# VectorE's weight step moved behind the work of its slot, and five smaller changes, in a four-layer model on one core

## What is computed

```python
def rms_norm(x, g):
    y = xf * lax.rsqrt(jnp.mean(xf * xf, axis=-1, keepdims=True) + EPS)
    return (y * g).astype(x.dtype)

def layer_c(...):                                   # layer 1
    u, gate = jnp.split(rms_norm(x, norm_g) @ w_in, 2, axis=-1)
    z = jax.nn.gelu(s5_ssm(u, ...))
    z = z * jax.nn.sigmoid(z @ glu_w + glu_b)
    return x + (z * jax.nn.silu(gate)) @ w_out

def first_block(...): ...                           # layers 0 and 1
    return rms_norm(x, final_norm_g)

def second_block(...):                              # layers 2 and 3
    for l in range(DEPTH):
        proj = jnp.einsum("bsd,de->bse", rmsnorm(x, norm_w[l]), w_in[l])
        ...                                         # ssd, conformer and attention branches
        x = x + jnp.einsum("bse,ed->bsd", concatenate([y_ssd, y_cfm, y_att]), w_out[l])

def ssd_chunked(x, dt, A, B, C):                    # 16 heads of 64, chunks of 128
    a_cs = jnp.cumsum(a, axis=-1)
    decay_in = segsum_exp(a_cs)
    y_diag = jnp.einsum("bcgls,bcgjls,bcsgjp->bclgjp", cb, decay_in, xdt)
```

## Time and profile before

| | us |
|---|---|
| median of three runs | 3628.29 |
| lowest and highest | 3622.89, 3630.3 |
| the profiled execution | 3625.47 |
| its span | 3623.7 |
| PE busy | 3464.2 |
| VectorE busy | 2127.2 |
| ACT busy | 1288.7 |
| GpSimd busy | 150.4 |

### The profile page before, as it was taken

One profiled execution on the slowest core, in us unless ns is written; L12 is line 12 of the kernel. 1 busy time (PEld: TensorE's weight loads), 2 busy tenths in 40 slices (PEclk: granted clock), 3 DMA queues, 4 the chain that ended last, 5 costly groups with the idle time before them and its releaser, 6 DMA issues.

```text
span 3623.7 us, 42976 instructions
## 1 busy us (share of the span) xinstructions
PE 3464.2 (96%) x15890; PEld 2770.9 (76%) x15890; DVE 2127.2 (59%) x3122; ACT 1288.7 (36%) x2013; POOL 150.4 (4%) x100
## 2 busy tenths in 40 slices
PE   8899999999999999999989999998999999999899
PEld 6687887777777888788878876776777887677677
DVE  6755546677655645434244775566755476565774
ACT  4233324444332233423152224324423223532442
POOL 2000000000020000000050000000002000000000
PEclk9899999999999999999999999998999999999899
DMA  4233335566665555645443442344446343334445
GB/s 163 100 123 123 112 130 180 175 235 217 227 212 183 177 176 185 202 168 198 152 161 117 164 137 99 114 139 164 151 160 216 106 166 132 104 122 161 141 156 198
DMA packets 286129, 574.58 MB, mean 159 GB/s; under 512 B 61392, under 2 KB 101088, under 8 KB 285408
## 3 DMA queue, kind: packets, MB, share of 16 engines
q1 hardware_dynamic: 285920, 571.83, 47.0%
HBM read 440.65 MB, written 131.07 MB: 158 GB/s over the span
## 4 chain that ended last, share of the span: by engine, by line
PE 52%; issue 23%; DVE 13%; ACT 6%; DMA 3%; DVEq 2%; POOLq 1%; SPq 0%; ACTq 0%
PE bank L542 34%; PE bank L541 11%; DVE weights_low L467 3%; ACT weights_high L394 2%; DVE arena L1963 2%; ACT arena L1905 1%; POOLq L453 1%; DVE residual_in L2037 1%; DVE arena L1958 1%; DMA convert_in<-x 1%; PE bank L1076 1%; DVEq L2541 1%; ACT arena L1902 1%; DVE act_low L525 1%; PE bank L988 1%
## 5 line engine op out<-in xcount | busy, mean ns | idle before, releaser
L542 PE MATMUL bank<-act_high,weights_high 128*128 128x512 f32 x3584 | 1449.3, 404 | 77.1 <-DVE stream_out L514 34.7
L542 PE MATMUL bank<-act_low,weights_high 128*128 128x512 f32 x3584 | 1416.8, 395 | 0.0
L467 DVE TENSOR_TENSOR weights_low<-weights_raw,weights_high 128x1024 fp32r<-128x1024 f32 x528 | 656.9, 1244 | 1122.0 <-ACT weights_high L394 1119.4
L394 ACT ACTIVATE weights_high<-weights_raw 128x1024 fp32r<-128x1024 f32 x528 | 558.1, 1057 | 1517.7 <-PE bank L542 1256.4
L542 PE MATMUL bank<-act_high,weights_low 128*128 128x512 f32 x3584 | 962.8, 389 | 0.0
L542 PEld LDWEIGHTS bank<-act_high,weights_high 128*128 128x128 f32 x3584 | 686.1, 191 | 248.0 <-issue 54.4
L542 PEld LDWEIGHTS bank<-act_low,weights_high 128*128 128x128 f32 x3584 | 685.7, 191 | 138.5 <-issue 2.9
L542 PEld LDWEIGHTS bank<-act_high,weights_low 128*128 128x128 f32 x3584 | 672.8, 188 | 140.1
L541 PE MATMUL bank<-weights_high,act_high 128*128 128x512 f32 x640 | 255.4, 399 | 23.3 <-DVE stream_out L480 18.1
L541 PE MATMUL bank<-weights_high,act_low 128*128 128x512 f32 x640 | 250.6, 392 | 0.0
L2037 DVE SCALAR_TENSOR_TENSOR residual_in<-residual_in,arena 128x512 f32<-128x512 f32 x240 | 180.4, 752 | 20.8 <-issue 1.8
(11 more groups left out here) (318 smaller groups left out, 2879.4 us busy)
## 6 DMA issues: line engine op xcount, KB each, us to landing
weights_raw<-in_w_all SPq DMA_DIRECT2D x528, 512.0 KB, 3.3
convert_in<-mix SPq DMA_DIRECT2D x80, 256.0 KB, 4.2
fm_b<-stream_out SPq DMA_DIRECT2D x72, 256.0 KB, 2.3
mix<-arena SPq DMA_DIRECT2D x64, 256.0 KB, 2.7
x_part<-stream_out SPq DMA_DIRECT2D x48, 256.0 KB, 2.2
residual_in<-x_part SPq DMA_DIRECT2D x12, 1024.0 KB, 7.0
x<-stream_out SPq DMA_DIRECT2D x48, 256.0 KB, 2.6
convert_in<-x SPq DMA_DIRECT2D x48, 256.0 KB, 3.9
```

Source lines behind the costliest of these rows:

```text
L394: e.activation(WH[:, t % 3, :], RAW[:, t % 3, :], ACT.Copy).then_inc(wh_ready, 1)
L467: e.tensor_tensor(WL[:, t % 3, :], RAW[:, t % 3, :], WH[:, t % 3, :].bitcast(F32), ALU.subtract).then_inc(wl_ready, 1)
L542: return e.matmul(bank[s][:, :], a[:, s * P:(s + 1) * P], h, start=start, stop=stop)
```

## The change

1. VectorE's slot becomes: evacuation, converts, take(t), WL(t+2).
2. Ahead of layer 2 each tile is squared once. GpSimd adds the squares, and VectorE adds them times the square of the gain to the second sum, one operation for each tile.
3. The constants of S5 get buffers of their own, stand in 27 slots between 10 and 75, and GLA doesn't wait for them.
4. k of S5 is written to four groups of 32 partitions (columns of the array), and one ACT copy of 128x256 takes it out.
5. SSD: the cumulative sums of all heads are formed once for each layer; each head picks its row with one rounded matmul of 512 columns; y of a pair of heads is formed together, the instructions alternating between the two column halves; a head has six slots and four buffers of decay.
6. The residual is loaded tile by tile; where a pass with a residual follows another, each tile's load is issued right behind the store of the tile before.

```diff
-                if t + AHEAD < NU:
-                    weights_dve(e, t + AHEAD)
                 for n in BY_SLOT.get(t, ()):
                     convert_dve(e, n)
                 take(t)
+                if t + AHEAD < NU:
+                    weights_dve(e, t + AHEAD)
```

```diff
-                square_act(e, SQ_AT[ph] + (2 * k if ph == 5 else k), x)
-                if ph == 5:
-                    square_act(e, SQ_AT[ph] + 2 * k + 1, x, GAIN[:, 2, k:k + 1])
+                square_act(e, SQ_AT[ph] + k, x)
...
+            if ph == 5:
+                sq = SQ_AT[ph] + k
+                e.wait_ge(sq_ready, sq + 1)
...
+                    e.scalar_tensor_tensor(ACC2, SQ[:, sq % 2, :], GAIN[:, 6, k:k + 1], ACC2, ALU.mult, ALU.add
+                                           ).then_inc(sq_gained, 1)
```

```diff
-        PREP_STEPS = 12
+        PREP_SLOTS = [*range(10, 22), *range(29, 33), *range(43, 46), *range(56, 59), 69, 70, 71, 74, 75]
+        PREP_STEPS = len(PREP_SLOTS)
...
-                e.wait_ge(*pr_d.at("done"))
```

```diff
             for g in range(S5_G):
-                mm = e.matmul(mid[2 + g // 4][0:S5_C, (g % 4) * P:(g % 4 + 1) * P], sw_vb[:, g, P - S5_C:],
+                r = slice(32 * (g % 4), 32 * (g % 4) + 32)
+                mm = e.matmul(mid[2][r, (g // 4) * P:(g // 4 + 1) * P], sw_vb[:, g, P - 2 * S5_C:],
                               sw_cp[:, g, 0:P], start=True, stop=True)
```

```diff
-            for b in range(TB):
-                mm = e.matmul(mid[h % 2][:, b * P:(b + 1) * P], sd_ab[h % 2][:, b, :], TRI[:, :], start=True, stop=True)
...
+            e.matmul(mid[h % 2][:, :], SMW[:, h, :], ROWS_R[:, :], start=True, stop=True).then_inc(*sd_pacs.mark("acs"))
+            yield
+            yield
+            yield
+            if h % 2:
...
+                for b in range(TB):
+                    for n in (h - 1, h):
+                        r = slice(64 * (n % 2), 64 * (n % 2) + 64)
+                        mm = e.matmul(mid[2 + k % 2][r, b * P:], sd_xdt[:, b, n * 64:(n + 1) * 64], packed(sd_e[n % 4], b),
+                                      start=b == 0, stop=b == TB - 1)
```

```diff
                 e.dma_start(dst, OUTB[:, s, :]).then_inc(out_stored, 16)
+                if follows(q + 1):
+                    residual_sp(e, q + 1, s)
```

More of the change, by code:

```diff
@@ L960, in sw_act @@
                 e.wait_ge(sw_kst, 16 * b)
-            for n in range(2):
-                ins = e.activation(sw_k[0:S5_C, 4 * n:4 * n + 4, :],
-                                   mid[2 + n][0:S5_C, :].rearrange("p (g n) -> p g n", g=4), ACT.Copy)
-            ins.then_inc(*sw_a.mark("kc"))
+            e.activation(two_d(sw_k), mid[2][:, 0:2 * P], ACT.Copy).then_inc(*sw_a.mark("kc"))
             e.wait_ge(*sw_d.at("arg", b))
@@ L1675, in build @@
         sd_e = [A(PACK[4]) for _ in range(2)]
-        sd_ab = [A(TB, P) for _ in range(2)]
         sd_x, sd_z, sd_y = A(2, L), A(2, L), A(2, L)
@@ L1680, in build @@
         sd_w, sd_dsk, sd_pick = A(12, 5), A(8), A(16)
+        after_conv = Arena(0, 6 * L)
+        sd_e += [after_conv(PACK[4]) for _ in range(2)]
+        sd_two = sd_x[:, 0, :].rearrange("p (b n) -> p b n", b=TB)
         conv = Arena(SD_E, SD_E + 2 * PACK[4])
@@ L1710, in ssd_pre_pe @@
             e.matmul(mid[0][:, 0:64], TRI[:, :], a2, start=True, stop=True)
-            e.matmul(mid[0][:, 64:128], ONES[:, :], a2, start=True, stop=True).then_inc(*sd_tp.mark("sums"))
+            e.matmul(mid[0][:, 64:128], ONES[:, :], a2, start=True, stop=True)
+            for b in range(TB):
+                mm = e.matmul(mid[1][:, b * P:(b + 1) * P], sd_two[:, b, :], TRI[:, :], start=True, stop=True)
+            mm.then_inc(*sd_tp.mark("sums"))
             yield
@@ L1761, in ssd_pre_dve @@
                 e.drain()
-            e.drain().then_inc(*sd_td.mark("bias"))
+            e.tensor_copy(ROWS_R[:, :], mid[1][:, :])
+            e.drain()
+            low = slice(64, P)
+            e.tensor_tensor(ROWS_R[low, :], mid[1][low, :], ROWS_R[low, :].bitcast(F32), ALU.subtract)
+            e.drain().then_inc(*sd_td.mark("rows"))
             yield
@@ L1953, in ssd_dve @@
             e.wait_ge(*sd_pacs.at("acs", t))
-            ee, ps = sd_e[h % 2], mid[h % 2]
-            if h >= 2:
-                e.wait_ge(*sd_py.at("y", t - 2))
+            ee, ps = sd_e[h % 4], mid[h % 2]
+            if h >= 4:
+                e.wait_ge(*sd_py.at("y", l * 8 + k - 2))
+            if h == 2:
+                for n in range(2):
+                    e.wait_ge(sd_xst[n], 16 * (l * 4 + 4))
             for b in range(TB):
@@ L2577, in _ @@
                     weights_sp(e, t + 5)
-                if UNITS[t][0] in XR_TURN and FIRST[UNITS[t][0]] == t:
-                    residual_sp(e, UNITS[t][0])
+                q = UNITS[t][0]
+                if q in XR_TURN and FIRST[q] == t and not follows(q):
+                    residual_free_sp(e, q)
+                    for s in range(4):
+                        residual_sp(e, q, s)
                 for n in BY_SLOT.get(t + 1, ()):
```

182 lines of the change are left out of this document (104 added, 78 removed).

## The result

| | before, us | changed, us |
|---|---|---|
| median of four runs each | 3629.3 | 3683.7 |
| lowest and highest | 3622.9, 3630.7 | 3679.3, 3686.6 |
| span of the profiled execution | 3623.7 | 3677.5 |

The changed kernel takes 1.0152 times as long (95% interval 1.0135 to 1.017): slower by 54 us, where I had forecast slower by 21. The direction and the mechanism of the loss hold; the two large numbers whose difference I forecast were both too small.

What follows compares the result with a forecast made beforehand. The prediction took PE, busy 96% of the span, as the bound: 3625.5 us less 109 of gains plus 131 for serial loads gave 3647.5, forecast as 3650 with the median's 2.8 offset; own range 3630 to 3675, overall 3575 to 3695.

Steps and rivals of the forecast that it cites:

- The cost of serial loads: In converting slots, the next slot's convert loads wait on SP behind weights that wait for WL; +131 us.
- S5 constants: Spreading the S5 constants over 27 VectorE slots removes PE's 18.1 us evacuation wait and two cold starts; -25 us.
- k: S5's k matmuls in four column groups instead of one, overlapping only in part; -8 us, bounds 0 and -23.
- y: SSD heads' y alternating between two column halves of the array, overlapping in part; -29 us, bounds 0 and -37.
- The ratios that I took from the earlier trace: Row-half matmuls (L2245) against the same columns in sequence: 0.56 and 0.76; 0.61 taken for y, 0.76 for k.
- The rule of the Trainium skill that the prediction cites: Column tiles of PE's array operate independently and can run matmuls in parallel; would give y -37 and k -23 us.
- item 6: Mid steps and evacuations outside converting slots come up to 1.23 us earlier on VectorE; -8 us (0 to -15).
- items 2, 3, 5: SSD heads: cheaper sums (-20 us), y on alternating column halves (-29), shorter waits from an extra slot and four buffers (-15).
- Residual: Residual loads issued tile by tile, each right behind a store, save some of PE's evacuation waits at L514; -4 us.
- The full-overlap rival: Column tiles in y and k overlap completely, giving their full bounds: 3627 us, no change; chance 0.14.
- The rival that PE's own mid work pays for the chain: In convert groups, mid steps overlap the next slot's load latency, so serial loads cost +66: 3585 us; chance 0.34.
- The rival that column halves take turns: Column tiles in y and k don't overlap, so both give nothing: 3687 us; chance 0.14.

Runs made afterwards that it cites:

- loads first: Changed kernel, VectorE's new order kept, with SP issuing the next slot's convert loads ahead of the weights and residual; 3474.4 us, ratio 0.9578.

## Why the prediction was wrong in size

- **The cost of serial loads, predicted +131, measured +209** (3683.7 - 3474.4). This is the step that failed. The mechanism, its place in SP's queue and the stretches were right; the period and the number of slots were not. By stretch, changed against loads first, with what was predicted in brackets: 104 to 112 +28 (24), 200 to 216 +21.6 (16), 264 to 280 +28.6 (12), the first layer +17.8 (9), 112 to 136 +20 (8, as single converts), 136 to 152 +15.6 (8), 232 to 248 +14.0 (11), both attention stretches +47 (24), 392 to 408 +15.7 (10). Three reasons show: I counted only the six slots of a pair of converts ahead of a pass, while what follows them (the sum of squares, L624, the mid steps) is late as well; the 5.9 us from the end of WL to the second low part became 8.2 in slot 204 (1511.34 to 1519.57), presumably because mid steps issue transfers of their own there; and in slots 267 to 271 GpSimd's adds hold VectorE, 10.9 us for the 9.4 worked out.
- **The gains, predicted -109, measured -155** (span 3468.5 against 3623.7, with the cost away). Item by item: S5 constants -24 (predicted -25). k: 16 x 1.27 = -20 on PE (-8), because four column groups overlap fully. y: 2.30 less per pair, 16 pairs = -37 on PE (-29); the undoing cost 29, since one head after the other still overlaps a little. The ratios that I took from the earlier trace rows weren't shares of overlap. There too the two instructions of a pair start within 0.01 us of each other, but a pair of 256 columns stands 0.31 us from what follows it, where a single one of y with 256 columns stands 0.22: row halves carried some 0.1 us more for each pair, and column halves and quarters don't. The rule of the Trainium skill that the prediction cites was right here, by these traces in full: column tiles run in parallel.
- **The order by itself, predicted -8 (item 6), measured -51 on the kernel before and -67 on the changed one.** I priced it as 1.2 us per step, the length of WL. What it does is to open the circle of the SSD heads, in which VectorE was idle for 3.5 us ahead of each WL (4.0 in the kernel before) while its steps for the heads were ready. The 4.21 in the earlier trace rows is an idle time ahead of WL as well, but one in bare slots: there ACT waits for PE and nothing stands behind WL, so it costs nothing.
- **SSD** (items 2, 3, 5 together -64): measured -93.3 with the order and -24.6 without it. Taking PE's work away turned into waits for VectorE and ACT where the circle set the pace; "nothing else is late next" was wrong for the old order and right for the new.
- **Residual** (-4): its early issue cost 10.
- The full-overlap rival had the overlap right, and the "same" that it ended on wrong, since the chain cost more. The rival that PE's own mid work pays for the chain is refuted by the stretches of the table. The rival that column halves take turns named 3687, nearest of all to the 3683.7; that is luck, for its mechanism is refuted by the run with one head after the other.

So two errors of 78 and 46 us with opposite signs left one of 33; that the forecast came so near is luck.

## What to carry to other kernels

Before a step is moved on one engine, look at every queue that waits for its semaphore: here a transfer that another slot needed stood behind a wait for the moved step, and the place of two lines in SP's queue decided between 1.5% slower and 4.2% faster. Price an in-order step by the wait that it does as well as by its own length; the bracket of the timeline tells it. Then follow that wait back: if it leads through other engines to the step itself, the order is a circle with a period of its own, and the slowest circle sets the slot. Where a change has a clear mechanism for a loss, work it out over everything that runs late after it, not over the slots in which it acts.

## What the runs showed of the hardware that I had not expected

- Matmuls on different column halves or quarters overlap in full: 16 instructions of y in 2.30 us (8 before), and four of k in the 0.11 us of one. Two row halves also start together, but a pair of 256 columns took 0.31 us where one instruction of y took 0.22.
- A VectorE operation with its inputs in SBUF that starts while a GpSimd add runs ends no earlier than the add: 1.29 us for a copy of 128x8, and two-input operations 0.54 us behind it. One that reads a PSUM bank isn't held: 1.13 us for four of L2005 with or without an add.
